# Down weights as sixteen neighbouring rows a partition, with gate and up splits that read every sixteenth column

## The chip, the cores and the metric

The kernel runs on one core of one Trainium2 chip. The metric is the device time of one execution in microseconds (us). The profile names the engines PE (TensorE, the matrix engine; PEld is its weight load), DVE (VectorE), ACT (ScalarE), POOL (GpSimd) and SP (SyncE, which issues most transfers here). Transfers between HBM and the on-chip memory run on 16 DMA engines.

## The reference

One encoder layer over 528 tokens (16 meta tokens and 512 of input) of width 1024: retention and a Hyena convolution, mixed and added to the input, and then a mixture of experts with expert choice. The change lies in the experts:

```python
def expert_choice_moe(xn, w_router, w_gate, w_up, w_down):
    cap = EC_CAPACITY * T // N_EXPERTS          # 66 tokens for each of 16 experts
    aff = jax.nn.softmax(logits, axis=-1)
    gate, idx = lax.top_k(jnp.swapaxes(aff, 1, 2), cap)
    xe = xn[bidx, idx]
    hid = jax.nn.silu(jnp.einsum('becd,edf->becf', xe, w_gate)) * jnp.einsum('becd,edf->becf', xe, w_up)
    ye = jnp.einsum('becf,efd->becd', hid, w_down) * gate[..., None].astype(xn.dtype)
    return jnp.zeros_like(xn).at[bidx, idx].add(ye)
```

For each expert, `w_gate` and `w_up` are 1024 x 2048 and `w_down` is 2048 x 1024, all in f32, 8 MB each. The sum over the 2048 hidden features f may be taken in any order, as long as `hid` and `w_down` agree on it.

## The kernel before

The products run in f16 with three terms. Each f32 weight is scaled and split into a high part (`wh`, ACT) and a low part (`wl`, DVE, scaled weight minus high part), and PE multiplies low by high, high by high and high by low.

The expert weights come in chunks of 2 MB: four for gate, four for up and four for down in each expert, so 192 chunks in all. SP loads them into six slots (`slot`, 128 partitions x 4096 f32) and issues the next load of a slot when DVE has split what was in it (`load`, lines 405 to 407). A gate or up chunk holds two neighbouring rows of 2048 columns for each partition, 16 KB that lie together in HBM. A down chunk holds four rows of 1024 columns for each partition. They are 128 rows apart in HBM, so each partition reads four runs of 4 KB:

```python
return w_down[e].rearrange("(t p) n -> p t n", p=128)[:, 4 * q:4 * q + 4, :]
```

ACT splits off the high part of a chunk into a ring of four buffers (`high`, line 699; `high_first`, line 693, for the first expert's gate and up chunks), DVE follows with the low part (`low`, line 1139; `low_first`, line 1075). Then PE uses the chunk and frees its ring buffer (`chunk_used`). Every queue works in program order.

The expert stage is a loop of rounds. Round e (1 to 15) handles the gate chunks (c = 0 to 3) and up chunks (4 to 7) of expert e and then the down chunks (8 to 11) of expert e - 1. DVE's round is twelve `low`, with the low half of `hidt` after the fourth (line 1151), then `gated` (line 1147, three instructions) and `split_x` (line 1134, two). ACT's round is twelve `high`, with the output of the expert before (line 714) and the high half of `hidt` (line 709) after the fourth, the silu (line 705) before the eighth, and `evac_x` (line 686) at the end. Four of the first expert's eight chunks are split already in the stage before, that of the output projection `w_o`, between the steps of `h_add` (line 1083); PE waits for these steps before it reuses the result banks. The last expert's down chunks come after the rounds, from `hidt_end` (lines 709 and 1151) on.

`project_x` (lines 1494 to 1509) multiplies a gate or up chunk: for each of its two rows kk and each of 16 tiles t of hidden features it loads 128 weights from column `f = FF * kk + 128 * t` of the ring buffer. Tile t so holds the features 128 t to 128 t + 127. `down` (lines 1511 to 1523) takes row s of chunk q as tile t = 4 q + s of the hidden features.

Of the kernel before, what the change touches and what calls it, by code (L numbers as in the profile page):

```python
# [9 lines left out]
ALU = mybir.AluOpType  # L10
ACT = mybir.ActivationFunctionType
# [4 lines left out]
E, FF = 16, 2048  # L16
# [19 lines left out]
W_S = 2.0 ** 8  # L36
# [40 lines left out]
RING = 4  # L77
SLOTS = 6
# [116 lines left out]
def build(nc, A, out, xt_rows, xn2_rows, h_rows):  # L195
    ctx = ExitStack()
    with ctx:
# [12 lines left out]
        S = {n: ctx.enter_context(nc.semaphore("s_" + n)) for n in SEMS}  # L210
# [123 lines left out]
            return w_up[e].rearrange("(p k) n -> p k n", k=KD)[:, 2 * q:2 * q + 2, :]  # L334

        def down_src(e, q):
            return w_down[e].rearrange("(t p) n -> p t n", p=128)[:, 4 * q:4 * q + 4, :]

        def slot_dst(n, rows):
            return slot[n % SLOTS][:, :].rearrange("p (k n) -> p k n", k=rows)  # L340
# [173 lines left out]
        def _(act):  # L514
# [62 lines left out]
            for hf in range(2):  # L577
                for part in range(3):
                    for c in range(2):
                        if part != 2 or c:  # L580
                            raw_hi(6 * hf + 2 * part + c + 2)
                        for i in (2 * c, 2 * c + 1):
# [7 lines left out]
                            if part == 2:  # L590

                                n = 4 * hf + i
# [95 lines left out]
            def high_first(c):  # L688

                act.wait_ge(slot_in[c % SLOTS], 16 * (c // SLOTS + 1))  # L690
                if c >= RING:
                    act.wait_ge(S["chunk_used"], c - RING + 1)
                nc.scalar.activation(wh[c % RING][:, :], slot[c % SLOTS][:, :], ACT.Copy, scale=W_S).then_inc(S["w_hi"], 1)  # L693

            def high(e, c):

                act.wait_ge(slot_in[(c + 2) % SLOTS], e * 32 + 16 * ((c + 2) // SLOTS))
                act.wait_ge(S["chunk_used"], e * MOE_CH + c - RING - 3)
                nc.scalar.activation(wh[c % RING][:, :], slot[(c + 2) % SLOTS][:, :], ACT.Copy, scale=W_S).then_inc(S["w_hi"], 1)  # L699

            def silu(done):

# [92 lines left out]
            nc.scalar.activation(warm[:, :], ones[0:1, 0:8], ACT.Sqrt).then_inc(S["warm"], 1)  # L795
            hidt_high(E - 1, hidt_end)
            for c in range(4):
                high(E, c)
                if c == 3:
                    ye_out(E - 2, E * MOE_CH - 4, 3072)  # L800
            ye_out(E - 1, E * MOE_CH, 1536)
# [11 lines left out]
        def _(dve):  # L813
# [258 lines left out]
            def low_first(c):  # L1072

                dve.wait_ge(S["w_hi"], c + 1)
                nc.vector.scalar_tensor_tensor(wl[c % RING][:, :], slot[c % SLOTS][:, :], W_S, wh[c % RING][:, :],  # L1075
                                               ALU.mult, ALU.subtract).then_inc(S["w_lo"], 1)

            raw_lo(C_O + 2)
# [54 lines left out]
                    src = ps_all[:, 1536 + 512 * b:1536 + 512 * b + 4 * CAP].rearrange("p (k c) -> p k c", k=4)  # L1133
                    nc.vector.tensor_tensor(xcur[:, 4 * b:4 * b + 4, 1, :], src, xcur[:, 4 * b:4 * b + 4, 0, :], ALU.subtract).then_inc(S["xcur_lo"], 1)

            def low(e, c):

                dve.wait_ge(S["w_hi"], e * MOE_CH + c - 3)
                nc.vector.scalar_tensor_tensor(wl[c % RING][:, :], slot[(c + 2) % SLOTS][:, :], W_S, wh[c % RING][:, :],  # L1139
                                               ALU.mult, ALU.subtract).then_inc(S["w_lo"], 1)  # L1140

            def gated(done, freed):

# [27 lines left out]
            moe(E - 1, True)  # L1171
            hidt_low(E - 1, hidt_end)
            for c in range(4):
                low(E, c)
            dve.wait_ge(S["gf_row"], 16)
            for k in range(1, NT):
                dve.wait_ge(S["fin_root"], k)
# [5 lines left out]
        def _(pe):  # L1183
# [310 lines left out]
            def project_x(q, freed):  # L1494

                i = q % RING
                for kk in range(2):
                    k = 2 * q + kk
                    for t in range(16):
                        if k == 0 and t % TIL == 0 and freed is not None:  # L1500
                            pe.wait_ge(S["psum_free"], freed + t // TIL)
                        f = FF * kk + 128 * t
                        hi, lo = wh[i][:, f:f + 128], wl[i][:, f:f + 128]
                        at = tile_at(t)
                        dst = ps_all[:, at:at + CAP]
                        nc.tensor.matmul(dst, lo, xcur[:, k, 0, :], start=k == 0 and t % TIL == 0, stop=False, skip_group_check=True)  # L1506
                        nc.tensor.matmul(dst, hi, xcur[:, k, 0, :], start=False, stop=False, skip_group_check=True)  # L1507
                        last = nc.tensor.matmul(dst, hi, xcur[:, k, 1, :], start=False, stop=k == KD - 1, skip_group_check=True)  # L1508
                last.then_inc(S["chunk_used"], 1)
# [153 lines left out]
```

## Time and profile before

| | |
|---|---|
| median of 3 runs | 1826.54 us (1825.85 to 1828.33) |
| the profiled execution | 1827.22 us |
| its span, first to last instruction | 1825.2 us |
| mean granted TensorE clock | 0.936 of full speed |
| PE, DVE, ACT, POOL busy | 83%, 71%, 55%, 15% of the span |
| read from HBM | 470.24 MB, 265 GB/s over the span |

The profile is of one execution. Busy shares are averages over stages of different kinds; the chain that ended last is followed back from the last instruction, at each step to what released it. A row of the queue's timeline gives the start, the length, the engine and line, and in brackets how long the engine was idle before and what ended the wait.

### The profile page before, as it was taken

The page shows a single profiled execution, that of the slowest core. Times are in us where ns is not written, and L with a number is a line of the kernel's source. Part 1 is how long each engine was busy: PE and PEld are TensorE (multiplying, and loading weights), DVE is VectorE, ACT ScalarE, POOL GpSimd, SP SyncE. Part 2 cuts the span into 40 slices and gives each one's busy share as a digit, 9 for nine tenths or more (in the row PEclk, how much of TensorE's full clock was granted, in tenths as well). Part 3 has the DMA queues.
Part 4 walks back from the last instruction along what each step waited for, and adds up shares of the span by engine and source line. Part 5 has one row for each costly group of instructions (what it writes and reads, how often), then busy time and mean ns, then how long its engine had stood idle before and what let it go on. Part 6 is the DMA issues. An engine that isn't in the chain of part 4 may idle for free.

```text
span 1825.2 us, 42918 instructions
## 1 busy us (share of the span) xinstructions
PE 1509.5 (83%) x19515; PEld 1168.5 (64%) x19515; DVE 1292.1 (71%) x782; ACT 1010.1 (55%) x639; POOL 279.0 (15%) x150
## 2 busy tenths in 40 slices
PE   5999999999999999746886687678768767876874
PEld 3657757886788887646666466656656564665652
DVE  3756556633533344747998988998988889889984
ACT  5433423331332224446777777776777777777773
POOL 1243243300000000220471001010100011010000
PEclk7999999999999999868998998998989989989997
DMA  9303103330037421748999999999999999999993
GB/s 328 107 1 105 47 1 115 93 93 0 24 149 244 140 93 53 279 155 314 413 397 413 406 410 397 416 413 399 403 416 410 395 414 408 405 396 418 425 403 114
DMA packets 109830, 484.29 MB, mean 265 GB/s; under 512 B 6187, under 2 KB 51563, under 8 KB 93052
## 3 DMA queue, kind: packets, MB, share of 16 engines
q1 hardware_dynamic: 103584, 467.18, 65.2%
q0 software_dynamic: 5472, 15.67, 3.1%
q8 instruction: 62, 1.02, 0.2%
q10 hardware_dynamic: 700, 0.33, 0.1%
q14 instruction: 12, 0.10, 0.0%
HBM read 470.24 MB, written 12.91 MB: 265 GB/s over the span
## 4 chain that ended last, share of the span: by engine, by line
DMA 35%; PE 33%; DVE 15%; ACT 9%; issue 4%; POOL 3%; ACTq 0%; SPq 0%; DVEq 0%; POOLq 0%
PE ps_all L1200 23%; DMA slot<-in_w_exp_gate 17%; DMA slot<-in_w_exp_down 16%; DVE wl L1139 10%; ACT wh L699 6%; PE ps_all L1320 3%; PE ps_all L1223 2%; PE ps_all L1363 1%; PE ps_all L1308 1%; DVE wl L1075 1%; POOL qk L464 1%; DMA xn_rows<-xb 1%; DMA h_rows<-ye,tok 1%; ACT wh L693 1%; DVE wsp L826 1%
## 5 line engine op out<-in xcount | busy, mean ns | idle before, releaser
L1139 DVE SCALAR_TENSOR_TENSOR wl<-slot,wh 128x4096 f16<-128x4096 f32 x184 | 809.4, 4422 | 101.7 <-ACT wh L699 101.3
L699 ACT ACTIVATE wh<-slot 128x4096 f16<-128x4096 f32 x184 | 664.3, 3616 | 229.4 <-DMA slot<-in_w_exp_down 107.5
L1506 PE MATMUL ps_all<-xcur,wl 128*128 128x66 f16 x4096 | 422.5, 198 | 195.5 <-ACT sg L705 108.3
L1506 PEld LDWEIGHTS ps_all<-xcur,wl 128*128 128x128 f16 x4096 | 398.2, 103 | 206.8 <-ACT sg L705 106.3
L1508 PE MATMUL ps_all<-xcur,wh 128*128 128x66 f16 x4096 | 421.9, 201 | 2.7 <-issue 2.7
L1507 PE MATMUL ps_all<-xcur,wh 128*128 128x66 f16 x4096 | 422.2, 199 | 0.7 <-issue 0.7
L1507 PEld LDWEIGHTS ps_all<-xcur,wh 128*128 128x128 f16 x4096 | 398.3, 100 | 2.8 <-issue 2.7
L1508 PEld LDWEIGHTS ps_all<-xcur,wh 128*128 128x128 f16 x4096 | 398.3, 101 | 2.8 <-issue 2.8
L1200 PE MATMUL ps_all<-xnt,wsp 128*128 128x272 f16 (+1 forms) x2688 | 307.6, 277 | 0.0
L1200 PEld LDWEIGHTS ps_all<-xnt,wsp 128*128 128x128 f16 x2688 | 263.4, 98 | 45.1 <-issue 4.7
L1520 PE MATMUL ps_all<-wh,hidt 128*66 128x512 f16 x480 | 181.8, 379 | 23.6 <-DVE wl L1139 23.6
L826 DVE SCALAR_TENSOR_TENSOR wsp<-raw,wsp 128x2048 f16<-128x2048 f32 x44 | 102.8, 2337 | 137.4 <-ACT wsp L529 137.1
L1522 PE MATMUL ps_all<-wh,hidt 128*66 128x512 f16 x480 | 181.9, 379 | 0.0
L1521 PE MATMUL ps_all<-wl,hidt 128*66 128x512 f16 x480 | 181.9, 379 | 0.0
L495 POOL DMA_INDIRECT h_rows<-ye,tok x16 | 98.0, 6126 | 526.7 <-ACT ye L714 526.7
L529 ACT ACTIVATE wsp<-raw 128x2048 f16<-128x2048 f32 x44 | 83.7, 1901 | 79.2 <-PE ps_all L1200 50.6
L1520 PEld LDWEIGHTS ps_all<-wh,hidt 128*66 128x66 f16 x480 | 53.1, 111 | 79.8 <-issue 34.1
L488 POOL DMA_INDIRECT xg<-xn_rows,tok x16 | 32.0, 1997 | 357.9 <-PE ps_all L1489 357.0
L1522 PEld LDWEIGHTS ps_all<-wh,hidt 128*66 128x66 f16 x480 | 53.2, 111 | 50.4
L1521 PEld LDWEIGHTS ps_all<-wl,hidt 128*66 128x66 f16 x480 | 53.2, 111 | 45.7
L470 POOL TENSOR_TENSOR sqa<-sqa,sqt 128x528 f32<-128x528 f32 x6 | 7.8, 1307 | 382.0 <-ACT sqt L736 382.0
L1223 PE MATMUL ps_all<-wsp,xnt 128*128 128x256 f16 (+1 forms) x480 | 53.5, 273 | 0.8 <-ACT v L637 0.8
(234 smaller groups left out, 1599.4 us busy)
## 6 DMA issues: line engine op xcount, KB each, us to landing
slot<-in_w_exp_gate SPq DMA_DIRECT2D x64, 2048.0 KB, 24.0
slot<-in_w_exp_up SPq DMA_DIRECT2D x64, 2048.0 KB, 21.4
slot<-in_w_exp_down SPq DMA_DIRECT2D x64, 2048.0 KB, 22.8
raw<-in_w_in SPq DMA_DIRECT2D x32, 1024.0 KB, 5.8
raw<-in_w_ret_out SPq DMA_DIRECT2D x4, 1024.0 KB, 12.9
raw<-in_w_hy_out SPq DMA_DIRECT2D x4, 1024.0 KB, 8.6
raw<-in_w_o SPq DMA_DIRECT2D x4, 1024.0 KB, 5.3
win_t<-in_c_win SPq DMA_DIRECT2D x2, 1536.0 KB, 10.9
```

What stands on the lines that cost most here:

```text
L495: pool.indirect_dma_start(h_rows[:, :], bass.IndirectOffsetOnAxis(ap=tok[:, e:e + 1], axis=0), ye[:, :], None, compute_op=ALU.add).then_in ...
L699: nc.scalar.activation(wh[c % RING][:, :], slot[(c + 2) % SLOTS][:, :], ACT.Copy, scale=W_S).then_inc(S["w_hi"], 1)
L826: nc.vector.scalar_tensor_tensor(wsp[n % 3][:, 1, :, :], raw[n % 3][:, :, :], W_S, wsp[n % 3][:, 0, :, :], ALU.mult, ALU.subtract).then_in ...
L1139: nc.vector.scalar_tensor_tensor(wl[c % RING][:, :], slot[(c + 2) % SLOTS][:, :], W_S, wh[c % RING][:, :], ALU.mult, ALU.subtract).then_in ...
L1200: last = nc.tensor.matmul(pair(n, c, c + b - a, p), l, r[:, a:b], start=i == 0, stop=i == len(terms) - 1)
L1223: last = nc.tensor.matmul(pair(n, 0, CW, p), l, r, start=i == 0, stop=i == 3 * KD - 1)
L1506: nc.tensor.matmul(dst, lo, xcur[:, k, 0, :], start=k == 0 and t % TIL == 0, stop=False, skip_group_check=True)
L1507: nc.tensor.matmul(dst, hi, xcur[:, k, 0, :], start=False, stop=False, skip_group_check=True)
L1508: last = nc.tensor.matmul(dst, hi, xcur[:, k, 1, :], start=False, stop=k == KD - 1, skip_group_check=True)
L1520: nc.tensor.matmul(dst, l[0], wh[i][:, f:f + 512], start=t == 0, stop=False)
L1521: nc.tensor.matmul(dst, l[0], wl[i][:, f:f + 512], start=False, stop=False)
L1522: last = nc.tensor.matmul(dst, l[1], wh[i][:, f:f + 512], start=False, stop=t == 15)
```

## The change

The down chunks read other rows of HBM: partition p gets the rows 16 p + 4 q to 16 p + 4 q + 3, which are neighbours (16 KB in one run). Row t of partition p is then hidden feature 16 p + t. So that `hid` agrees with that, tile t of gate and up takes the features t, 16 + t, 32 + t and so on. That reordering is done in the splits of ACT and DVE: for gate and up chunks they read every sixteenth f32 of the slot (64 bytes apart) and write the f16 result in order, tile after tile. The splits of down chunks stay as they were (`c < 8 and not end` picks the gate and up chunks).

```diff
         def down_src(e, q):
-            return w_down[e].rearrange("(t p) n -> p t n", p=128)[:, 4 * q:4 * q + 4, :]
+            return w_down[e].rearrange("(p t) n -> p t n", t=16)[:, 4 * q:4 * q + 4, :]
+
+        def by_tile(ap):
+            return ap.rearrange("p (m t) -> p t m", t=16)
+
+        def in_tiles(ap):
+            return ap.rearrange("p (t m) -> p t m", t=16)
...
-                nc.scalar.activation(wh[c % RING][:, :], slot[c % SLOTS][:, :], ACT.Copy, scale=W_S).then_inc(S["w_hi"], 1)
-
-            def high(e, c):
+                nc.scalar.activation(in_tiles(wh[c % RING][:, :]), by_tile(slot[c % SLOTS][:, :]), ACT.Copy, scale=W_S).then_inc(S["w_hi"], 1)
+
+            def high(e, c, end=False):
 
                 act.wait_ge(slot_in[(c + 2) % SLOTS], e * 32 + 16 * ((c + 2) // SLOTS))
                 act.wait_ge(S["chunk_used"], e * MOE_CH + c - RING - 3)
-                nc.scalar.activation(wh[c % RING][:, :], slot[(c + 2) % SLOTS][:, :], ACT.Copy, scale=W_S).then_inc(S["w_hi"], 1)
+                hi, r = wh[c % RING][:, :], slot[(c + 2) % SLOTS][:, :]
+                if c < 8 and not end:
+                    hi, r = in_tiles(hi), by_tile(r)
+                nc.scalar.activation(hi, r, ACT.Copy, scale=W_S).then_inc(S["w_hi"], 1)
...
-                high(E, c)
+                high(E, c, True)
...
-                nc.vector.scalar_tensor_tensor(wl[c % RING][:, :], slot[c % SLOTS][:, :], W_S, wh[c % RING][:, :],
+                nc.vector.scalar_tensor_tensor(in_tiles(wl[c % RING][:, :]), by_tile(slot[c % SLOTS][:, :]), W_S, in_tiles(wh[c % RING][:, :]),
                                                ALU.mult, ALU.subtract).then_inc(S["w_lo"], 1)
...
-            def low(e, c):
+            def low(e, c, end=False):
 
                 dve.wait_ge(S["w_hi"], e * MOE_CH + c - 3)
-                nc.vector.scalar_tensor_tensor(wl[c % RING][:, :], slot[(c + 2) % SLOTS][:, :], W_S, wh[c % RING][:, :],
-                                               ALU.mult, ALU.subtract).then_inc(S["w_lo"], 1)
+                lo, r, hi = wl[c % RING][:, :], slot[(c + 2) % SLOTS][:, :], wh[c % RING][:, :]
+                if c < 8 and not end:
+                    lo, r, hi = in_tiles(lo), by_tile(r), in_tiles(hi)
+                nc.vector.scalar_tensor_tensor(lo, r, W_S, hi, ALU.mult, ALU.subtract).then_inc(S["w_lo"], 1)
...
-                low(E, c)
+                low(E, c, True)
...
-                        f = FF * kk + 128 * t
+                        f = 256 * t + 128 * kk
```

## Rows read from the trace of the kernel before

**Rows 1.** The page: busy us of each engine, share of the span.

```profile
PE 1509.5 (83%) x19515; PEld 1168.5 (64%) x19515; DVE 1292.1 (71%) x782; ACT 1010.1 (55%) x639; POOL 279.0 (15%) x150
```

**Rows 2.** The page: the chain that ended last, by engine and by line.

```profile
DMA 35%; PE 33%; DVE 15%; ACT 9%; issue 4%; POOL 3%; ACTq 0%; SPq 0%; DVEq 0%; POOLq 0%
PE ps_all L1200 23%; DMA slot<-in_w_exp_gate 17%; DMA slot<-in_w_exp_down 16%; DVE wl L1139 10%; ACT wh L699 6%; PE ps_all L1320 3%; PE ps_all L1223 2%; PE ps_all L1363 1%; PE ps_all L1308 1%; DVE wl L1075 1%; POOL qk L464 1%; DMA xn_rows<-xb 1%; DMA h_rows<-ye,tok 1%; ACT wh L693 1%; DVE wsp L826 1%
```

**Rows 3.** Busy time by stretch; last come granted clock, DMA share, GB/s.

```profile
760.00:830.00 70.00, 33.98 (x731) 32.10 (x730) 40.79 (x62) 28.28 (x23) 19.38 (x18) 0.68 0.63 243
...
965.00:1030.00 65.00, 50.05 (x906) 38.93 (x904) 57.02 (x19) 47.91 (x20) 5.51 (x2) 0.91 1.02 409
1030.00:1096.00 66.00, 50.51 (x961) 39.34 (x958) 59.39 (x20) 50.85 (x22) 5.56 (x3) 0.95 1.01 409
1096.00:1160.00 64.00, 49.48 (x897) 38.35 (x894) 56.34 (x19) 47.34 (x20) 5.96 (x3) 0.92 1.02 407
```

**Rows 4.** ACT in order of time, one round: start, length, what it waited for.

```profile
991.59 3.62 ACT L699 ACTIVATE wh<-slot 128x4096 f16<-128x4096 f32 x1 [1.59 <-DMA slot<-in_w_exp_down]
...
1001.83 3.62 ACT L699 ACTIVATE wh<-slot 128x4096 f16<-128x4096 f32 x1 [1.50 <-DMA slot<-in_w_exp_down]
1009.21 3.62 ACT L699 ACTIVATE wh<-slot 128x4096 f16<-128x4096 f32 x1 [3.77 <-DMA slot<-in_w_exp_down]
1012.74 0.65 ACT L686 ACTIVATE xcur<-ps_all 128x264 f16<-128x264 f32 x2
1014.30 3.62 ACT L699 ACTIVATE wh<-slot 128x4096 f16<-128x4096 f32 x1 [0.92 <-DMA slot<-in_w_exp_gate]
...
1028.98 3.62 ACT L699 ACTIVATE wh<-slot 128x4096 f16<-128x4096 f32 x1 [1.27 <-DMA slot<-in_w_exp_gate]
1032.50 1.10 ACT L714 ACTIVATE ye<-ps_all,gate 66x1024 f32<-66x1024 f32 x1
1033.50 1.07 ACT L709 ACTIVATE hidt<-hid 128x1056 f16<-128x1056 f32 x1
```

**Rows 5.** DVE in order of time over the same round.

```profile
1017.21 1.38 DVE L1147 SCALAR_TENSOR_TENSOR hid<-ps_all,sg 128x396 f32<-128x396 f32 x3
1018.50 0.76 DVE L1134 TENSOR_TENSOR xcur<-ps_all,xcur 128x264 f16<-128x264 f32 x2
1019.18 13.08 DVE L1139 SCALAR_TENSOR_TENSOR wl<-slot,wh 128x4096 f16<-128x4096 f32 x3
...
1036.97 1.25 DVE L1151 TENSOR_TENSOR hidt<-hid,hidt 128x1056 f16<-128x1056 f32 x1
...
1047.31 4.43 DVE L1139 SCALAR_TENSOR_TENSOR wl<-slot,wh 128x4096 f16<-128x4096 f32 x1 [0.42 <-ACT wh L699]
```

**Rows 6.** The DVE splits of `slot`: ns min/median/max, first and last start.

```profile
L1139 DVE SCALAR_TENSOR_TENSOR wl<-slot,wh x184: 4411/4424/4475, 840.2 to 1790.3; 128x4096 f16<-128x4096 f32 x184
```

**Rows 7.** DVE in order of time at the end of the rounds.

```profile
1773.79 1.26 DVE L1151 TENSOR_TENSOR hidt_end<-hid,hidt_end 128x1056 f16<-128x1056 f32 x1 [1.15 <-ACT hidt_end L709]
```

**Rows 8.** DMA queue of SP: packets, MB, share of 16 engines.

```profile
q1 hardware_dynamic: 103584, 467.18, 65.2%
```

**Rows 9.** Groups by line and form: busy us, mean ns, idle before.

```profile
L1489 PEld LDWEIGHTS ps_all<-ident,xg 66*128 66x128 f32 x128 | 15.4, 202 | 12.1 <-issue 12.1
L1446 PEld LDWEIGHTS ps_all<-ident,ht 128*128 128x128 f32 x32 | 6.6, 224 | 0.1
L470 POOL TENSOR_TENSOR sqa<-sqa,sqt 128x528 f32<-128x528 f32 x6 | 7.8, 1307 | 382.0 <-ACT sqt L736 382.0
```

**Rows 10.** DVE in order of time, the end of the w_o stage.

```profile
703.12 2.29 DVE L826 SCALAR_TENSOR_TENSOR wsp<-raw,wsp 128x2048 f16<-128x2048 f32 x1 [1.09 <-ACT wsp L529]
...
721.26 4.41 DVE L1075 SCALAR_TENSOR_TENSOR wl<-slot,wh 128x4096 f16<-128x4096 f32 x1
725.60 0.69 DVE L1083 SCALAR_TENSOR_TENSOR ht<-ps_all,ht 128x528 f32<-128x528 f32 x1
...
748.09 4.43 DVE L1075 SCALAR_TENSOR_TENSOR wl<-slot,wh 128x4096 f16<-128x4096 f32 x1 [3.33 <-ACT wh L693]
```

## The prediction, made before the change was run

> **What bounds the kernel now.** I read the page's busy shares first. No engine fills the span: PE is busy for 83% of it, DVE for 71%, ACT for 55% [rows 1]. An average over unlike stages does not say what sets the end, so the chain that ended last comes next: DMA has the largest share, 35%, and 33 points of that are the loads of `slot` from the expert weights; the DVE split of line 1139 has 10% and the ACT split of line 699 6% [rows 2]. Then the busy time by stretch inside the expert stage: in three neighbouring stretches the 16 DMA engines are busy the whole time (share 1.01 to 1.02) and move 407 to 409 GB/s, while DVE works 57.0 of 65.0 us, 59.4 of 66.0 and 56.3 of 64.0, nine tenths of the time [rows 3]. The stage is bound by DMA, and the engine next behind it, by a small margin, is DVE.
>
> The ACT queue in order of time shows the rhythm of the loads, because almost every split of ACT starts at the landing it waited for. The four splits that wait for gate chunks start from 1014.30 to 1028.98: 14.68/3 = 4.89 us apart. The first three that wait for down chunks start from 991.59 to 1001.83: 10.24/2 = 5.12 us apart. Each chunk is 2 MB, so that is 429 and 410 GB/s. The fourth down split starts 7.38 us after the third: there the transfers of the POOL queue take their share [rows 4].
>
> DVE's own cost is read from its queue. Three splits back to back take 13.08 us, so one takes 4.36 us from start to start; the gating takes 1.29 (1017.21 to 1018.50), the split of the gathered rows 0.68 (1018.50 to 1019.18), and the low half of `hidt` 1.17 (1036.97 to 1038.14) [rows 5]. A round of one expert has twelve chunks: 12 x 4.36 + 3.14 = 55.5 us of DVE work. The fifteen rounds run from the first line-1139 split at 840.2 [rows 6] to the `hidt_end` split at 1773.8 [rows 7], 933.6 us, or 62.2 us each. So DVE has 6.7 us of slack in a round, 0.84 us for each of its eight gate and up chunks. ACT's round is 12 x 3.62, plus 1.10 and 1.07 at line 714 and 709, about 1.2 for the silu and 0.65 for `xcur`: 47.4 us [rows 4], slack 14.8.
>
> **The change part by part.**
>
> *Down loads.* A down chunk's 128 partitions now read four neighbouring rows each, 16 KB in one run, where they read four rows of 4 KB. That is exactly the shape of a gate or up chunk (two neighbouring rows of 8 KB), so the price is in the trace: 4.89 in place of 5.12 us, 0.23 us a chunk. For 64 down chunks: 14.7 us off the DMA time, if DMA stays the bound. Packets on the page should fall, since three quarters of the 32,768 pieces of 4 KB go (64 x 512); they are a large part of the 103,584 packets of q1 [rows 8]. Number and order of DMA issues stay the same.
>
> *Addresses on PE.* Line 1502 now finds tile t of row kk at 256 t + 128 kk. Each weight block is still 128 neighbouring f16, so PE loads it as before: nothing, whatever else happens. Tile t now holds hidden columns t, 16+t, 32+t and so on, and partition p of a down chunk holds rows 16p+t, so `hidt` meets its rows without more work.
>
> *Gate and up splits, ACT.* Of 192 splits, 128 now read f32 words 64 bytes apart (256 of them in each of 16 passes) and write f16 in order. The `end` chunks and all down chunks stay contiguous.
>
> *Gate and up splits, DVE.* The same 128 chunks read the strided f32 `slot` as first source; the second source `wh` and the result `wl` are contiguous. No instruction is added. All hangs on what a strided word costs, and no DVE or ACT instruction in the trace has such a read. I bound it by the nearest rows. Below: today's rate, 4.42 us for 4096 elements [rows 6], nothing added, if a word has the same cost wherever it lies. The one group of the trace whose reads step over more than a neighbour is the weight load of the expert's gathered rows (`xg`, every eighth f32, 32 bytes): 202 ns for 128 columns, 1.58 ns a column, fixed part included. The contiguous f32 load of `ht` takes 224 ns for as many [rows 9]. So PE shows no penalty, but it also reads f32 no faster than that, and a penalty up to 1.58 ns would be hidden there. For DVE, at 4.27/4096 = 1.04 ns (4.42 less a fixed 0.15, an estimate from 4096 elements in 4.42 and 2048 in 2.29 [rows 6, 10], whose difference is 1.04 ns an element), 1.58 ns would be 2.2 us more a chunk. Above: the slowest plain f32 stream over SBUF in the trace, POOL's addition of line 470, 1307 ns for 528, 2.48 ns an element [rows 9]: 5.9 us more a chunk. Between these I take a word that costs one access of its own beside the element's cycle, so twice 1.04 ns: 4.27 us more a chunk, which is about midway between 1.58 and 2.48. I keep nothing as a possible price too, and bound the range by 2.2 and 5.9.
>
> The Trainium skill speaks to this. Its page "Vector Engine (DVE) Microarchitecture Reference", section 5.2, says that a port streams at full rate only while its elements come in runs of at least two adjacent 4-byte words, and gives 1.73 ns a column for one source that hops every element and 2.50 for both sources stepping 24 words. By 1.73 the sum below would end at 2110 us, by 2.50 at about 2510. No run here shows it; the contiguous splits agree with its 1.04 ns.
>
> **The sum.** With x us more for each strided chunk, a DVE round is 55.5 + 8x. It passes the 62.2 us of today when x is over 0.84, or 0.2 ns a word. At x = 4.27 it is 89.6 us, and DVE is the bound; I add 1.5 us a round for waits of DVE that do not vanish (estimate: today DVE waits 0.4 to 0.7 us for ACT several times a round [rows 5]). ACT, if a strided word costs it twice what it pays now (3.62 us a chunk), goes to 47.4 + 8 x 3.62 = 76 us and stays below DVE. The faster down loads are then worth nothing: DMA needs 61 of 91 us.
> - Fifteen rounds: 15 x (91.1 - 62.2) = +433 us.
> - First expert's eight chunks, lines 693 and 1075. Four lie in the w_o stage, where DVE starts the first of them at 721.26 without a wait, takes up `h_add`, for which PE waits, right behind it at 725.60, and waits only 3.33 us before the fourth [rows 10]; the other four are DVE's only work before the first gating. 8 x 4.27 = +34 us.
> - The tail from `hidt_end` on reads only contiguous down chunks: 0.
>
> The sum is +467 on the profiled execution's 1827.2 us (span 1825.2 and 2.0 around it), which is 0.7 above the median of 1826.5: 2294, said as **2290 us**. At x = 2.2 it is 15 x (74.6 - 62.2) + 18 = +204: 2031. At x = 5.9 it is 15 x (104.2 - 62.2) + 47 = +677: 2504.
>
> **Rivals.**
> - *Strided reads are free and the loads gain.* DMA stays the bound, 64 x 0.23 = 14.7 us go, rounds take 61.3 us, and DVE's 55.5 fit: 1812 us. For it: PE's load of `xg` is no slower than the contiguous one [rows 9], and DVE takes its element per cycle with f32 and f16 operands alike. Against it: PE's row is too slow to show a penalty, and DVE tolerates only 0.2 ns a word; this rival decides below that point. 11%. A rule speaks for it as well: "VectorE: DVE Perf Modes" in the Trainium skill, section on Mode 1×, says that this mode makes no assumptions and works with weird strides, at one result a cycle. DVE's 1.04 ns an element is that rate, for contiguous reads; by that rule the time would be this rival's.
> - *Free reads, no gain from the larger pieces*, or a stride price close to 0.2 ns that eats the gain: 1827 us. The measured 4.89 against 5.12 speaks against the first, the narrow window against the second. 4%.
> - *PE becomes the bound.* With rounds of 90 us PE works in bursts with pauses. Between 760 and 830 us, where it is busy for 34.0 of 70 us, its granted clock is 0.68, in the later stretches at 0.91 to 0.95 [rows 3]. If it sinks to the lower level of 1.2 GHz, a round's PE work of about 48 us (50.05/65 x 62.2, at 0.91) becomes 87 us, and with PE's waits for the silu between gate and up and for `hidt` (8 us, estimate) 95: 15 x (95 - 62.2) + 34 = +526, 2353 us. Or ACT is hit harder than DVE and its round of 47.4 + 8y passes DVE's; at y = 8 that is 111.4 us, 15 x (111.4 - 62.2) + 34 = +772, 2599 us. Together 15%.
> - The forecast, DVE bound by the strided reads, with x between 2.2 and 5.9: 70%.
>
> **How the numbers follow.** Most of the chance lies on slower. The range is 2030 to 2510 us: the two bounds of x, which also hold the case of the slow PE clock. It leaves out the two fast rivals (15%) and the dearest ACT case (some 5%). A measurement of this kernel can tell about 0.2% (4 us) from no change. Faster 0.11, same 0.04, slower 0.85; every priced stride above 0.2 ns is slower by far more than 4 us.
>
> **What would show it.** In the changed profile the 128 gate and up splits stand as a form of their own: DVE about 8.7 us (6.6 to 10.3), ACT about 7 us, while 64 down splits stay at 4.4 and 3.6. Rounds of about 91 us; DMA share in the stage near 0.7 and 280 GB/s; no wait of ACT for a `slot` DMA; DVE busy without gaps; PE waits for DVE's `wl`. The packets of q1 fall by some 24,000. I am wrong if the strided splits keep 4.4 us: then the loads of down should land 4.9 us apart and the time is 1812. I am wrong in size if x is not near 4.3, which the mean of the strided splits says directly, and wrong in the bound if DVE still idles more than a few us a round, which would point to ACT or to PE's clock.

## The result: 2097 us, 14.7% slower

The changed kernel takes 2097.21 us (median of 4 runs, 2093.11 to 2099.32) against 1826.95 of before in the same comparison: ratio 1.1473, 95% interval 1.1454 to 1.1491. Its profiled execution spans 2094.8 us, 269.6 more than the 1825.2 of before.

The page of the changed kernel, first busy time, then the DMA queue of SP, then the chain:

```profile
PE 1601.8 (76%) x19515; PEld 1262.7 (60%) x19515; DVE 1639.3 (78%) x782; ACT 1459.9 (70%) x639; POOL 514.5 (25%) x150
...
q1 hardware_dynamic: 79008, 467.18, 59.2%
...
ACT 29%; PE 28%; DVE 15%; issue 14%; DMA 10%; POOL 3%; DVEq 0%; ACTq 0%; POOLq 0%
```

Beside [rows 1] DVE has 347 us more and ACT 450 us more. Beside [rows 2] DMA has gone from 35% to 10% of the chain and ACT from 9% to 29%; what ACT's share means is said below, with its queue. Beside [rows 8] the queue moved the same bytes in 24,576 fewer packets.

The splits of `slot` in the changed kernel (ns min/median/max, first and last start):

```profile
L708 ACT ACTIVATE wh<-slot x184: 3599/7237/7647, 858.9 to 2054.0; 128x4096 f16<-128x4096 f32 x184
L1151 DVE SCALAR_TENSOR_TENSOR wl<-slot,wh x184: 4415/7168/7422, 865.9 to 2060.1; 128x4096 f16<-128x4096 f32 x184
```

Two kinds of split are mixed in each row. The shortest are those of the down chunks, as long as in [rows 4, 6]; the medians of the rows fall among the gate and up splits: DVE 7.17 us where it was 4.42, ACT 7.24 where it was 3.62. The 120 gate and up splits by themselves have medians of 7.22 and 7.27 us. From start to start they are 7.09 us apart on DVE (four of them from 1022.79 to 1051.15 in the queue below), where it was 4.36, so 2.73 us more.

Three stretches of the expert stage (busy time of PE, PEld, DVE, ACT, POOL; clock, DMA share, GB/s), to be laid beside [rows 3]:

```profile
970.00:1050.00 80.00, 55.07 (x892) 44.11 (x888) 79.15 (x19) 76.51 (x20) 37.28 (x3) 0.83 0.86 331
1050.00:1130.00 80.00, 54.67 (x877) 43.86 (x878) 79.13 (x20) 76.51 (x20) 30.35 (x3) 0.83 0.85 324
1130.00:1210.00 80.00, 56.17 (x915) 45.30 (x913) 79.16 (x20) 76.54 (x21) 30.35 (x3) 0.82 0.86 325
```

DVE is busy for 79.1 of 80 us and ACT for 76.5; the DMA engines, full before, now have a pause. DVE's queue over one round and at the end of the rounds, beside [rows 5, 7]:

```profile
1022.11 0.83 DVE L1143 TENSOR_TENSOR xcur<-ps_all,xcur 128x264 f16<-128x264 f32 x2
1022.79 28.55 DVE L1151 SCALAR_TENSOR_TENSOR wl<-slot,wh 128x4096 f16<-128x4096 f32 x4
1051.15 1.34 DVE L1162 TENSOR_TENSOR hidt<-hid,hidt 128x1056 f16<-128x1056 f32 x1
1052.33 21.57 DVE L1151 SCALAR_TENSOR_TENSOR wl<-slot,wh 128x4096 f16<-128x4096 f32 x3
1074.78 24.58 DVE L1151 SCALAR_TENSOR_TENSOR wl<-slot,wh 128x4096 f16<-128x4096 f32 x5 [0.87 <-ACT wh L708]
1099.24 1.41 DVE L1158 SCALAR_TENSOR_TENSOR hid<-ps_all,sg 128x396 f32<-128x396 f32 x3
1100.54 0.79 DVE L1143 TENSOR_TENSOR xcur<-ps_all,xcur 128x264 f16<-128x264 f32 x2
...
2043.56 1.26 DVE L1162 TENSOR_TENSOR hidt_end<-hid,hidt_end 128x1056 f16<-128x1056 f32 x1 [1.15 <-ACT hidt_end L718]
```

From one split of gathered rows to the next, 1022.11 to 1100.54, a round takes 78.4 us, with one wait of DVE, 0.87 us for ACT. The whole difference of the spans is in three pieces: the first split of the rounds starts at 865.9 and not at 840.2 (+25.7), the fifteen rounds from there to `hidt_end` take 1177.7 and not 933.6 us (+244.1), and the tail from `hidt_end` takes 51.2 and not 51.4 (-0.2). They add up to the 269.6.

ACT's queue over the same round:

```profile
1014.51 28.75 ACT L708 ACTIVATE wh<-slot 128x4096 f16<-128x4096 f32 x4 [1.91 <-PE ps_all L1533]
...
1086.82 3.62 ACT L708 ACTIVATE wh<-slot 128x4096 f16<-128x4096 f32 x1 [1.58 <-PE ps_all L1519]
```

ACT is idle twice, 3.5 us in all, each time until PE frees a ring buffer, and DVE once, 0.87 us. So DVE is the fuller of the two, although the chain gives ACT 29% and DVE 15%. The chain goes from each instruction back to what released it: a DVE split to ACT's split of the same chunk, an ACT split to a load or to PE, a load to a DVE split. Two engines that are almost full share it in this way, and its shares do not say which of them sets the round. Even loads are in it (8 of DMA's 10% are up chunks), though ACT was never idle for one before a split of the rounds. Which engine counts is settled by the runs with one strided engine below.

### The profile page after: what moved, and what is told of

It is laid out like the page before. It is cut to its first block, busy times and chain, and to the rows that moved or that the text cites. A ratio compares the mean times of both kernels' runs of the same rounds, so it can differ in the third digit from the quotient of the medians.

```text
span 2094.8 us, 42918 instructions
## 1 busy us (share of the span) xinstructions
PE 1601.8 (76%) x19515; PEld 1262.7 (60%) x19515; DVE 1639.3 (78%) x782; ACT 1459.9 (70%) x639; POOL 514.5 (25%) x150
## 4 chain that ended last, share of the span: by engine, by line
ACT 29%; PE 28%; DVE 15%; issue 14%; DMA 10%; POOL 3%; DVEq 0%; ACTq 0%; POOLq 0%
ACT wh L708 24%; PE ps_all L1211 20%; DVE wl L1151 10%; DMA slot<-in_w_exp_up 8%; PE ps_all L1331 2%; PE ps_all L1234 2%; DVE wl L1084 2%; PE ps_all L1374 1%; ACT wh L699 1%; PE ps_all L1319 1%; ACT ye L723 1%; ACT sg L714 1%; POOL qk L470 1%; ACT hidt L718 1%; DMA h_rows<-ye,tok 1%
## 5 line engine op out<-in xcount | busy, mean ns | idle before, releaser
L1151 DVE SCALAR_TENSOR_TENSOR wl<-slot,wh 128x4096 f16<-128x4096 f32 x184 | 1136.9, 6257 | 22.9 <-ACT wh L708 22.9
L708 ACT ACTIVATE wh<-slot 128x4096 f16<-128x4096 f32 x184 | 1089.7, 6024 | 51.3 <-PE ps_all L1533 26.7
L1517 PE MATMUL ps_all<-xcur,wl 128*128 128x66 f16 x4096 | 515.2, 214 | 396.4 <-DVE wl L1151 211.8
L1517 PEld LDWEIGHTS ps_all<-xcur,wl 128*128 128x128 f16 x4096 | 450.2, 113 | 411.2 <-ACT sg L714 165.9
L1518 PE MATMUL ps_all<-xcur,wh 128*128 128x66 f16 x4096 | 515.4, 215 | 0.0
L1519 PE MATMUL ps_all<-xcur,wh 128*128 128x66 f16 x4096 | 515.1, 216 | 0.0
L1519 PEld LDWEIGHTS ps_all<-xcur,wh 128*128 128x128 f16 x4096 | 450.9, 112 | 0.0
L1518 PEld LDWEIGHTS ps_all<-xcur,wh 128*128 128x128 f16 x4096 | 450.4, 112 | 0.0
L501 POOL DMA_INDIRECT h_rows<-ye,tok x16 | 204.7, 12793 | 443.1 <-ACT ye L723 443.1
L494 POOL DMA_INDIRECT xg<-xn_rows,tok x16 | 160.8, 10048 | 467.9 <-PE ps_all L1500 467.2
L1084 DVE SCALAR_TENSOR_TENSOR wl<-slot,wh 128x4096 f16<-128x4096 f32 x8 | 58.9, 7372 | 21.9 <-ACT wh L699 21.9
```

The lines of the kernel that those rows point to most:

```text
L494: pool.indirect_dma_start(xg[:, :], None, xn2_rows[:, :], bass.IndirectOffsetOnAxis(ap=tok[:, e:e + 1], axis=0)).then_inc(S["x_in"], 16)
L501: pool.indirect_dma_start(h_rows[:, :], bass.IndirectOffsetOnAxis(ap=tok[:, e:e + 1], axis=0), ye[:, :], None, compute_op=ALU.add).then_in ...
L708: nc.scalar.activation(hi, r, ACT.Copy, scale=W_S).then_inc(S["w_hi"], 1)
L1151: nc.vector.scalar_tensor_tensor(lo, r, W_S, hi, ALU.mult, ALU.subtract).then_inc(S["w_lo"], 1)
```

## The experiments

**The loads alone** (before, with only the new source of down):

```diff
-            return w_down[e].rearrange("(t p) n -> p t n", p=128)[:, 4 * q:4 * q + 4, :]
+            return w_down[e].rearrange("(p t) n -> p t n", t=16)[:, 4 * q:4 * q + 4, :]
```

> The kernel before with the new down source alone; the splits of gate and up stay contiguous, so hidden features and down rows do not match and the output is not the reference's. Theory (the loads of 16 KB pieces are faster, but the strided splits hide that): DMA stays the bound, 64 chunks land 0.23 us sooner, 1812 us (1808 to 1816), down landings 4.9 us apart. Rival (pieces of 4 KB and 16 KB load at the same rate; the 5.12 us of before had another cause): 1827 us, landings 5.1 apart.

Measured: 1813.79 us (5 runs), ratio 0.9932 (0.9918 to 0.9945). ACT in order of time in this kernel:

```profile
989.17 3.62 ACT L699 ACTIVATE wh<-slot 128x4096 f16<-128x4096 f32 x1 [1.36 <-DMA slot<-in_w_exp_down]
994.06 3.62 ACT L699 ACTIVATE wh<-slot 128x4096 f16<-128x4096 f32 x1 [1.28 <-DMA slot<-in_w_exp_down]
998.96 3.62 ACT L699 ACTIVATE wh<-slot 128x4096 f16<-128x4096 f32 x1 [1.28 <-DMA slot<-in_w_exp_down]
```

Down chunks now land 4.89 and 4.90 us apart, where they were 5.12 apart [rows 4]. The half of the change that concerns HBM does what it should, and is worth 0.7%.

**The splits alone** (the changed kernel with the old source of down):

```diff
-            return w_down[e].rearrange("(p t) n -> p t n", t=16)[:, 4 * q:4 * q + 4, :]
+            return w_down[e].rearrange("(t p) n -> p t n", p=128)[:, 4 * q:4 * q + 4, :]
```

> The changed kernel with the old down source; features and rows do not match, so the output is not the reference's. Theory (all of the loss is the price of strided words on DVE and ACT, and DMA has slack): within 0.3% of the changed kernel, 2092 to 2102 us, rounds of 78.4 us. Rival (the new loads have a part in the loss, by contention or by later landings): at least 10 us faster than 2097.

Measured: 2096.30 us (4 runs), ratio 1.1477 (1.1459 to 1.1494), and splits of 7.15 us (DVE) and 7.23 (ACT). It cannot be told from the whole change. So the loss is the splits' alone, and the faster loads are worth nothing beside them.

**One engine at a time.** In the first of these two kernels DVE reads contiguously, in the second ACT does, in the first expert's splits as well (these lines are left out here):

```diff
-                    lo, r, hi = in_tiles(lo), by_tile(r), in_tiles(hi)
+                    lo, r, hi = lo, r, hi
```

> The changed kernel, but DVE splits contiguously; only ACT reads every sixteenth word. Low parts are wrong, so the output is not the reference's. Theory A (DVE alone sets the round, 12 x 4.36 + 3.1 + 8 x 2.74 = 77.4 us, and ACT at 7.24 us a split only follows): without it the round falls to ACT's 47.4 + 8 x 3.6 = 76.3 us and little above, so about 2060 to 2070 us. Theory B (ACT's waits for PE at the end of a round set the 78.4 us): nothing is won, 2085 to 2097 us. Rival C (the price comes from both engines reading strided at once): ACT's split falls below 5.5 us and the time below 1900.

Measured: 2034.25 us (one run); ACT's splits 7.17 us, DVE's 4.42.

```diff
-                    hi, r = in_tiles(hi), by_tile(r)
+                    hi, r = hi, r
```

> The changed kernel, but ACT splits contiguously; only DVE reads every sixteenth word. High parts are in another order than low parts, so the output is not the reference's. Theory A (DVE alone sets the round): round of 77.4 to 78.4 us, 2080 to 2097 us, DVE splits at 7.17 us. Theory B (ACT sets the round through its waits): the round is DVE's own work without waits, 77.4 us, 2080 us. Rival C (contention of two strided readers): DVE's split below 5.5 us, time below 1900.

Measured: 2063.69 us (one run); DVE's splits 7.22 us, ACT's 3.62. (In this kernel high and low part still add up to the reordered weight, against what I expected, since DVE subtracts whatever high part stands there; only the rounding is coarser.) Busy time in one stretch of 200 us, first ACT strided, then DVE strided:

```profile
1000.00:1200.00 200.00, 129.32 (x2223) 102.92 (x2221) 146.11 (x50) 198.56 (x51) 20.83 (x5) 0.81 0.89 345
```

```profile
1000.00:1200.00 200.00, 145.79 (x2209) 114.46 (x2206) 200.00 (x49) 122.69 (x51) 165.81 (x7) 0.85 0.89 339
```

Each time the engine that reads with a step is busy to the brim (198.56 and 200.00 of 200). Rival C falls: an engine alone pays as much as both together, so the price is not contention of the two readers. The rounds are read from the first split of DVE in them to `hidt_end`: 853.2 to 1980.8 us for ACT alone, 75.2 a round, and 856.5 to 2011.8 for DVE alone, 77.0 a round. Both engines together need 78.5 (1177.7/15). So the two bounds lie side by side: of 270 us, taking the strided read from DVE gives back 63, from ACT 34.

Both times came out below what I expected. For ACT alone I had 2060 to 2070 us, about 30 too many: from start to start a strided split of ACT takes 7.1 us and its other instructions about 1 each, so ACT's round is 75 us and not 76.3, and the stage starts 12.7 us earlier than in the changed kernel. For DVE alone both theories had 2080 us or more. The round of 77 us was right for theory B (DVE's own work without waits). What I had left out is the start: the rounds begin 9.4 us earlier when ACT's first splits are short, and the tail is 1.4 us shorter.

**The step of the read.** A down chunk q can also take the rows 512 q + 4 p + s or 1024 g + 8 p + s, still four neighbours and 16 KB in a run; then the splits need only every fourth or every eighth word. With two runs of 8 KB every second is enough. The cuts below are against the changed kernel; `in_tiles` gets the same number as `by_tile`.

```diff
-            return w_down[e].rearrange("(p t) n -> p t n", t=16)[:, 4 * q:4 * q + 4, :]
+            return w_down[e].rearrange("(q p t) n -> q p t n", q=4, t=4)[q]
...
-            return ap.rearrange("p (m t) -> p t m", t=16)
+            return ap.rearrange("p (m t) -> p t m", t=4)
...
-                        f = 256 * t + 128 * kk
+                        f = 1024 * (t % 4) + 512 * kk + 128 * (t // 4)
```

> As the changed kernel, but with the down rows 512 q + 4 p + s, so that the splits of ACT and DVE read every fourth f32 (16 bytes apart). Theory A (every read that is no neighbour costs an access of its own): DVE and ACT at about 7.2 us a split, time about 2097. Theory B (the price rises with the distance, or needs 64 bytes to appear): 4.4 to 6 us a split and 1812 to 1990 us.

```diff
+            return w_down[e].rearrange("(g p t) n -> g p t n", g=2, t=8)[q // 2, :, 4 * (q % 2):4 * (q % 2) + 4, :]
...
+            return ap.rearrange("p (m t) -> p t m", t=8)
...
+                        f = 512 * (t % 8) + 256 * kk + 128 * (t // 8)
```

> As with every fourth, but the splits read every eighth f32 (32 bytes apart), and the down rows are 1024 g + 8 p + s. Theory (any step that leaves the 16 bytes at each word pays the same, about 0.7 to 0.75 ns on DVE): 7.1 to 7.6 us a split, 2095 to 2155 us. Rival (the price is one of a step of exactly 16 bytes, or falls steadily with the distance): DVE's split clearly outside 7.1 to 7.6 us.

```diff
+            return w_down[e].rearrange("(b p t) n -> p b t n", b=8, t=2)[:, 2 * q:2 * q + 2, :, :]
...
+            return ap.rearrange("p (m t) -> p t m", t=2)
...
+            if rows == 5:
+                return slot[n % SLOTS][:, :].rearrange("p (b t n) -> p b t n", b=2, t=2)
...
+                    load(e, 8 + q, down_src(e - 1, q), 5)
...
+                        f = 2048 * (t % 2) + 1024 * kk + 128 * (t // 2)
```

> Down chunks read two runs of 8 KB for each partition, rows 256 b + 2 p and the next, and the splits read every second f32 (8 bytes apart), so each 16 bytes are used twice. Theory A (two adjacent words are needed for the full rate): about 7.2 us a split, time about 2097. Theory B (two hits on the same 16 bytes are enough): 4.4 and 3.6 us a split, DMA bound, 1812 to 1822 us.

The splits of the three kernels, every fourth, every eighth and every second word (DVE and ACT in each):

```profile
L708 ACT ACTIVATE wh<-slot x184: 3599/7555/7857, 862.4 to 2107.8; 128x4096 f16<-128x4096 f32 x184
L1151 DVE SCALAR_TENSOR_TENSOR wl<-slot,wh x184: 4390/7508/7745, 869.9 to 2114.0; 128x4096 f16<-128x4096 f32 x184
```

```profile
L708 ACT ACTIVATE wh<-slot x184: 3599/7612/7820, 859.8 to 2109.3; 128x4096 f16<-128x4096 f32 x184
L1151 DVE SCALAR_TENSOR_TENSOR wl<-slot,wh x184: 4405/7566/7692, 867.3 to 2115.5; 128x4096 f16<-128x4096 f32 x184
```

```profile
L710 ACT ACTIVATE wh<-slot x184: 3599/3939/4111, 840.9 to 1778.4; 128x4096 f16<-128x4096 f32 x184
L1153 DVE SCALAR_TENSOR_TENSOR wl<-slot,wh x184: 4407/4425/4427, 844.7 to 1784.5; 128x4096 f16<-128x4096 f32 x184
```

| step of the f32 read | DVE split | ACT split | time |
|---|---|---|---|
| none [rows 4, 6] | 4.42 us | 3.62 | 1826 us |
| 8 bytes | 4.43 | 3.94 | 1821.36 |
| 16 bytes | 7.51 | 7.56 | 2150.68 |
| 32 bytes | 7.57 | 7.61 | 2150.93 |
| 64 bytes (the change) | 7.17 | 7.24 | 2097.21 |

The splits are medians of all 184, as in the rows; those of the gate and up chunks alone are up to 0.06 us longer. The times of the steps from 8 to 32 bytes are of one run each. For every fourth word theory A was right in kind, with 7.2 us and 2097 us too low.

The price is a cliff and not a slope. With two words used of each 16 bytes DVE pays nothing and ACT 0.3 us; with one it is all there, and the longer step of 64 bytes even costs a little less than 16 or 32. The kernel with the step of 8 bytes, 1821.36 beside 1825.19 of before, is too near to be called a gain from one run; its down chunks land 4.97 us apart.

The Trainium skill has two rules for this, and the step of 8 bytes tells them apart. "Advanced Engine Details and Errata", section SBUF Cachelines, says that at least two hits on the same 16 bytes are needed for the full rate: DVE's 4.43 us at 8 bytes and 7.51 at 16 agree. They would agree as well with a plain rule of distance, the full rate up to 8 bytes and the price beyond; a step of 12 bytes would tell the two apart, and none was run. "Vector Engine (DVE) Microarchitecture Reference", section 5.2, asks for two address-adjacent words; by it the step of 8 bytes should be dear, and it is not. Its 1.73 ns a column for one source that hops 4 KiB at every element is close to what the change shows with 64 bytes: (7.17 - 0.15)/4096 = 1.71 ns.

**The other side of the same instructions.** Slot read in order, results written with the step, here 512 bytes of f16 (DVE also reads `wh` with it):

```diff
-            return ap.rearrange("p (m t) -> p t m", t=16)
+            return ap.rearrange("p (m t) -> p m t", t=16)
...
-            return ap.rearrange("p (t m) -> p t m", t=16)
+            return ap.rearrange("p (t m) -> p m t", t=16)
```

> The changed kernel with the reordering moved to the other side of the same instructions: slot is read in order, and the f16 results are written (and the high part read back by DVE) with a step of 256 elements, 512 bytes. Theory (the price lies in the f32 read alone, as a write may be buffered): splits at 4.4 and 3.6 us, 1812 us. Rival (each port pays for words that share no 16 bytes with their neighbour): DVE and ACT at 7.2 us or more, since DVE now has two such streams; 2097 us or slower.

Measured: 3892.54 us (one run). The splits in it, and ACT's queue in a part of one round:

```profile
L708 ACT ACTIVATE wh<-slot x184: 3595/19832/23475, 981.2 to 3851.1; 128x4096 f16<-128x4096 f32 x184
L1151 DVE SCALAR_TENSOR_TENSOR wl<-slot,wh x184: 4393/19816/20993, 999.6 to 3857.2; 128x4096 f16<-128x4096 f32 x184
```

```profile
1625.69 2.58 ACT L723 ACTIVATE ye<-ps_all,gate 66x1024 f32<-66x1024 f32 x1
1626.99 2.23 ACT L718 ACTIVATE hidt<-hid 128x1056 f16<-128x1056 f32 x1
1627.96 60.33 ACT L708 ACTIVATE wh<-slot 128x4096 f16<-128x4096 f32 x3
1683.88 5.40 ACT L714 ACTIVATE sg<-ps_all 128x396 f32<-128x396 f32 x3
```

The rival was right in kind and far too low: 19.8 us a split, 4.8 ns an element. The two contiguous instructions have records of 2.58 and 2.23 us, where they had 1.10 and 1.07 [rows 4], but these records overlap: from start to start the first takes 1.30 us and the second 0.97, where it was 1.00 (1032.50 to 1033.50) and 0.97. So these two hold the queue hardly longer than before. The three behind them hold it for 3.6 us (to the next split, at 1687.47), where it was 1.0 in the changed kernel (1066.27 to 1067.30); whether they are slower or the split behind them waits is not shown. Which part of the 4.8 ns is the write of f16 and which the pattern of 512 bytes was not tried, nor one engine alone.

**PE as the one that reorders.** A weight load may read with a step too. Then no split changes, and the down chunks are read as in the change:

```diff
-                        f = FF * kk + 128 * t
-                        hi, lo = wh[i][:, f:f + 128], wl[i][:, f:f + 128]
+                        f = FF * kk + t
+                        hi, lo = wh[i][:, f:f + 16 * 127 + 1:16], wl[i][:, f:f + 16 * 127 + 1:16]
```

> The same reordering, done by PE: the splits of ACT and DVE stay contiguous and each weight load of gate and up reads every sixteenth f16 of the ring buffer (32 bytes apart), 128 columns; down loads as in the changed kernel. Theory (a strided word costs DVE and ACT an access of its own, but a weight load, seen at 1.58 ns a strided f32 column and 0.8 ns a contiguous f16 column, pays little or hides it behind the matmuls): 1812 us (1805 to 1825). Rival (PE pays about 1.7 ns a column as the other engines do, 220 ns for each of 96 loads a chunk): PE needs 21 us a gate or up chunk, rounds of 190 us, about 3750 us.

Measured: 1955.46 us (5 runs), ratio 1.0708 (1.0688 to 1.0727). With the rows 512 q + 4 p + s for down:

```diff
-                        f = FF * kk + 128 * t
-                        hi, lo = wh[i][:, f:f + 128], wl[i][:, f:f + 128]
+                        f = FF * kk + 512 * (t // 4) + t % 4
+                        hi, lo = wh[i][:, f:f + 4 * 127 + 1:4], wl[i][:, f:f + 4 * 127 + 1:4]
```

> A down chunk q reads rows 512 q + 4 p to 512 q + 4 p + 3, also 16 KB in one run; then tile t of gate and up needs only every fourth feature of its block of 512, and PE reads its weights 8 bytes apart. Theory (the step does not matter to PE): 1812 us, as with every sixteenth. Rival (a weight load pays by the number of 16-byte lines it touches): slower than before, but less than with 32 bytes; with the lines at 2 columns each about half of that run's loss.

Measured: 1811.76 us (4 runs, 1810.43 to 1813.18), ratio 0.9919 (0.9898 to 0.9941): **0.8% faster than the kernel before**, as much as the loads alone gave. Unlike that run it does not leave out the matching order of the hidden features, so it is a full repair of the change. And with the rows 1024 g + 8 p + s:

```diff
+                        f = FF * kk + 1024 * (t // 8) + t % 8
+                        hi, lo = wh[i][:, f:f + 8 * 127 + 1:8], wl[i][:, f:f + 8 * 127 + 1:8]
```

> PE reads its weights of gate and up every eighth f16, 16 bytes apart, so that no two share 16 bytes; splits contiguous. Theory (the rule of two hits on the same 16 bytes holds for PE's weight loads too): as with every sixteenth, weight loads of 168 ns, PE the bound, 1955 us. Rival (PE's price follows the distance, so between 118 ns at 8 bytes and 168 at 32): weight loads near 140 ns, 1812 to 1880 us.

Measured: 1928.99 us (one run). One weight load of line 1508 in the kernel before, with every fourth, every eighth and every sixteenth column (ns min/median/max):

```profile
L1508 PEld LDWEIGHTS ps_all<-xcur,wh x4096: 95/96/136, 800.2 to 1754.1; 128*128 128x128 f16 x196
```

```profile
L1508 PEld LDWEIGHTS ps_all<-xcur,wh x4096: 111/118/136, 799.2 to 1741.7; 128*128 128x128 f16 x196
```

```profile
L1508 PEld LDWEIGHTS ps_all<-xcur,wh x4096: 157/163/176, 800.7 to 1864.6; 128*128 128x128 f16 x196
```

```profile
L1508 PEld LDWEIGHTS ps_all<-xcur,wh x4096: 158/166/187, 800.1 to 1890.8; 128*128 128x128 f16 x196
```

With two f16 columns used of each 16 bytes the record of a load is 118 ns long in place of 96, with one 163 or 166. A record is not what a load costs, though, since several are under way at once. Three in a row, in the kernel before and with every sixteenth column:

```profile
1025.00 0.10 PEld L1508 LDWEIGHTS ps_all<-xcur,wh 128*128 128x128 f16 x1
1025.03 0.10 PEld L1506 LDWEIGHTS ps_all<-xcur,wl 128*128 128x128 f16 x1
1025.06 0.10 PEld L1507 LDWEIGHTS ps_all<-xcur,wh 128*128 128x128 f16 x1
```

```profile
1025.01 0.16 PEld L1508 LDWEIGHTS ps_all<-xcur,wh 128*128 128x128 f16 x1
1025.07 0.16 PEld L1506 LDWEIGHTS ps_all<-xcur,wl 128*128 128x128 f16 x1
1025.14 0.16 PEld L1507 LDWEIGHTS ps_all<-xcur,wh 128*128 128x128 f16 x1
```

Loads start about 31 ns apart in the kernel before, 33 with every fourth column, 60 with every eighth and 62 with every sixteenth (mean over the 96 loads of a chunk in which PE does not pause). So every fourth column costs PE some 2 or 3 ns a load, and the large step lies where it lies on DVE and ACT, between 8 and 16 bytes. At 33 ns PE still has room. A stretch of 200 us, every fourth and then every sixteenth:

```profile
1000.00:1200.00 200.00, 164.15 (x2685) 125.24 (x2683) 180.11 (x61) 150.28 (x62) 26.86 (x7) 0.94 1.01 411
```

```profile
1000.00:1200.00 200.00, 198.22 (x2560) 172.59 (x2560) 159.05 (x53) 133.61 (x56) 18.94 (x6) 0.97 0.95 365
```

In the first DMA is the bound (share 1.01) and PE is busy for 164 of 200 us; in the second PE is, with 198.2, and the time is lost there. Of my two expectations for every sixteenth column neither held. The theory had the load free. The rival had 220 ns a load, one after the other, 21 us a chunk; even with the true 166 ns that sum would give 16 us, where 96 loads 62 ns apart take 6.0. For every fourth column the theory's time, 1812 us, came true and its reason did not: the loads do pay, as the rival said, but little and behind DMA. For every eighth the theory held, if a little less than with every sixteenth.

## Why the prediction came out as it did

*The bound.* DVE was forecast as the bound, with rounds of 55.5 + 8x and a little waiting. This held: at the measured x = 7.17 - 4.42 = 2.74 us (2.73 from start to start) DVE's work is 77.4 us, the round 78.4, and DVE waits 0.87 in it. Had I put 2.74 into the sum, with the 1.5 us of waits, it would have given 15 x (78.9 - 62.2) + 8 x 2.74 = +272, 2099 us, against the measured 2097.

*The size.* The term that was wrong is the price of a strided word: I took twice DVE's 1.04 ns, 4.27 us more a chunk, and it is 0.67 ns more, 2.74 us. That made the forecast 2290 us and not 2100; the measured time lies near the lower end of the range, 2030 to 2510. The step of the reasoning that failed is the one from rows that have no strided read of DVE to a price for one. The addition of POOL at 2.48 ns [rows 9] says something of POOL and nothing of a step. The load of `xg`, 1.58 ns a column [rows 9], looks closer to the truth (1.71 ns), but that is luck, as I had divided the length of a record that overlaps with the next ones:

```profile
998.50 0.96 PEld L1489 LDWEIGHTS ps_all<-ident,xg 66*128 66x128 f32 x8
```

Eight loads with records of 0.20 us take 0.96 us together, so they start 0.11 us apart, about 0.85 ns a column, which is less than DVE's 1.04 and would have bounded nothing. For ACT I had taken twice its present cost, 7.24 us a split, and that is what was measured. It is luck too, since the same rule of twice failed on DVE. In time both engines pay nearly the same, 7.22 and 7.27 us for 4096 words, although their contiguous rates differ.

*Three terms.* Rounds +244 us where +433 was said, the first expert's chunks +25.7 where +34 was said, the tail 0 as said. The start comes out closer to its forecast than the rounds do: 8 x 2.74 would be 21.9 us, and the other 3.8 are mostly a longer wait for ACT before the fourth split in the w_o stage, 6.85 us where it was 3.33 [rows 10]. ACT's longer split is on the path there, which I had not priced.

```profile
757.85 7.01 DVE L1084 SCALAR_TENSOR_TENSOR wl<-slot,wh 128x4096 f16<-128x4096 f32 x1 [6.85 <-ACT wh L699]
```

*ACT.* I put ACT at 76 us, 14 behind DVE's 90. It is at 75, and DVE came down to 77, so ACT is 2 us behind. The runs with one strided engine show what that means: neither repair alone gives back more than 63 of the 270 us.

*The loads.* 0.23 us a chunk and 14.7 us in all were forecast for them if DMA stayed the bound. Alone they gave 1813.8 us where 1812 was said, and in the changed kernel nothing, as said: the DMA share is 0.86 and no ACT split waits for a load. (0.7 and 280 GB/s were said, for rounds of 91 us.)

*The rivals.* Free reads: refuted on every engine, except for a step of 8 bytes on DVE. A low PE clock as the bound: the granted clock is 0.82 to 0.83, below the 0.91 to 0.95 of [rows 3] but far from the lower level, and PE is busy for 55 of 80 us. ACT hit harder than DVE: in proportion yes (twice against 1.6 times), but its round stays below DVE's.

What stays open is why 64 bytes are a little cheaper than 16 or 32 (7.17 against 7.51 and 7.57 on DVE), whether the cliff is one of 16-byte pieces or of distance, and what makes strided writes so dear.

## What to carry to other kernels

A better shape for a transfer that has to be paid for by a strided read elsewhere is a trade between a DMA term and an engine term: here 0.23 us a chunk in 64 chunks against 2.74 and 3.62 us a chunk in 128. Look first for the smallest reordering that gives the same transfer (here every fourth row and not every sixteenth), and count its step in bytes: every fourth f32 is 16 bytes and cost DVE and ACT the full price, every fourth f16 is 8 bytes, and PE's weight loads took it for 2 or 3 ns each, unseen behind DMA. Read the rate of an engine from start to start, since records can overlap: a strided load of PE has a record of 166 ns and comes every 62. When two engines carry the same burden, measure each alone before you repair one.

## What the runs showed that I had not expected

- The cliff lies between one and two words used of each 16 bytes, for f32 on DVE (4.43 to 7.51 us) and ACT (3.94 to 7.56), and for f16 weight loads on PE (33 to 60 ns from start to start).
- Writing f16 with a step of 512 bytes, on both engines at once, costs 4.8 ns an element (19.8 us a split).
- POOL's issue of an indirect transfer takes much longer in some of these kernels. The same group in the changed kernel, and with DVE alone strided, where DVE is busy for 200 of 200 us:

```profile
L501 POOL DMA_INDIRECT h_rows<-ye,tok x16 | 204.7, 12793 | 443.1 <-ACT ye L723 443.1
```

```profile
L501 POOL DMA_INDIRECT h_rows<-ye,tok x16 | 908.3, 56766 | 187.8 <-ACT ye L723 187.8
```

56.8 us each against 12.8; with ACT alone strided, where DVE is busy for 146 of 200 us, it is 4.2, and 6.1 in the kernel before. Among these four the issue takes longer where DVE has less idle time. That this is the cause was not tested, and it cannot be all: with strided writes the mean is 35.4 us, though DVE is busy for 189 of 200 us there and for 198 in the changed kernel. In neither kernel did PE or DVE wait for this group in the rounds; with DVE alone strided ACT did three times, 1.5 us in all.
